# Second down projection of a decoder layer: 16 of 22 k tiles as seven block products

## The reference

```python
def swiglu(x, w_gu, w_down):
    g, u = jnp.split(x @ w_gu, 2, axis=-1)
    return (jax.nn.silu(g) * u) @ w_down

x = x + 0.5 * rms_norm(swiglu(rms_norm(x, pre1), w1_gu, w1_down), post1)
...
x = x + 0.5 * rms_norm(swiglu(rms_norm(x, pre2), w2_gu, w2_down), post2)
```

## Time and profile before

| what | value |
|---|---|
| median of 3 runs | 1167.69 us (1166.46 to 1169.09) |
| the profiled execution | 1168.13 us |
| its span in the trace | 1166.4 us |
| granted TensorE clock, mean | 0.997 of full speed |
| first down stage | about 240 to 360 us |
| second down stage | about 1041 to 1161 us |

### The profile page before, as it was taken

One profiled execution on the slowest core, in us unless ns is written; L12 is line 12 of the kernel. 1 busy time (PEld: TensorE's weight loads), 2 busy tenths in 40 slices (PEclk: granted clock), 3 DMA queues, 4 the chain that ended last, 5 costly groups with the idle time before them and its releaser, 6 DMA issues.

```text
span 1166.4 us, 18885 instructions
## 1 busy us (share of the span) xinstructions
PE 1148.1 (98%) x7220; PEld 1005.9 (86%) x7220; DVE 711.3 (61%) x1153; ACT 519.0 (44%) x972; POOL 94.7 (8%) x198
## 2 busy tenths in 40 slices
PE   8999999999999999999999999999999999999998
PEld 7889999988887888888877888887889999998886
DVE  5888888843316445436886444746598888873233
ACT  6255555632227112247777222335435555552223
POOL 0000000073005100000031100002000000000002
PEclk9999999999999999999999999999999999999999
DMA  7323333347435433471200322232232333342321
GB/s 217 108 66 96 101 101 107 109 164 226 150 108 137 119 97 108 122 240 37 76 3 3 108 72 95 104 108 73 72 108 73 109 108 108 108 147 88 108 72 73
DMA packets 138559, 123.40 MB, mean 106 GB/s; under 512 B 4212, under 2 KB 125212, under 8 KB 138476
## 3 DMA queue, kind: packets, MB, share of 16 engines
q1 hardware_dynamic: 134304, 108.02, 30.7%
q0 software_dynamic: 4080, 14.50, 4.0%
q10 hardware_dynamic: 112, 0.03, 0.0%
HBM read 118.08 MB, written 8.90 MB: 109 GB/s over the span
## 4 chain that ended last, share of the span: by engine, by line
PE 95%; DVE 2%; ACT 1%; issue 1%; DMA 1%; SPq 0%; DVEq 0%; ACTq 0%
PE ps L1793 28%; PE ps L1900 28%; PE ps L1933 21%; PE ps L2038 4%; PE ps L2333 4%; PE ps L2317 2%; PE ps L2169 1%; PE ps L2191 1%; PE ps L2305 1%; PE ps L2100 1%; PE ps L2110 1%; PE ps L2121 1%; ACT p_n L1066 1%; PE ps L2139 1%; PE ps L1817 1%
## 5 line engine op out<-in xcount | busy, mean ns | idle before, releaser
L1190 DVE TENSOR_TENSOR ring_lo<-ring_raw,ring_hi 128x2048 fp32r<-128x2048 f32 (+1 forms) x54 | 121.5, 2252 | 187.4 <-ACT ring_hi L776 187.4
L776 ACT ACTIVATE ring_hi<-ring_raw 128x2048 fp32r<-128x2048 f32 (+1 forms) x54 | 101.5, 1882 | 236.7 <-PE ps L1933 142.0
L1793 PE MATMUL ps<-xn_hi,ring_hi 128*128 128x512 f32 x480 | 189.8, 395 | 2.3 <-DVE xn_lo L1215 2.3
L1793 PE MATMUL ps<-xn_hi,ring_lo 128*128 128x512 f32 x480 | 187.6, 391 | 0.0
L1793 PE MATMUL ps<-xn_lo,ring_hi 128*128 128x512 f32 x480 | 187.5, 391 | 0.0
L1900 PE MATMUL ps<-s_hi,ring_hi 128*128 128x256 f32 x512 | 144.9, 283 | 0.0
L1900 PE MATMUL ps<-s_lo,ring_hi 128*128 128x256 f32 x512 | 144.9, 283 | 0.0
L1900 PE MATMUL ps<-s_hi,ring_lo 128*128 128x256 f32 x512 | 144.9, 283 | 0.0
L1933 PE MATMUL ps<-ring_hi,h_hi 128*128 128x512 f32 x352 | 137.0, 389 | 0.0
L1933 PE MATMUL ps<-ring_hi,hT_lo 128*128 128x512 f32 x352 | 137.0, 389 | 0.0
L1933 PE MATMUL ps<-ring_lo,h_hi 128*128 128x512 f32 x352 | 136.9, 389 | 0.0
(11 more groups left out here) (298 smaller groups left out, 2078.1 us busy)
## 6 DMA issues: line engine op xcount, KB each, us to landing
ring_raw<-in_ffn_w_gu SPq DMA_DIRECT2D x86, 512.0 KB, 4.9
ring_raw<-in_ffn_w_down SPq DMA_DIRECT2D x44, 512.0 KB, 4.2
ring_raw<-in_w_in SPq DMA_DIRECT2D x42, 512.0 KB, 4.7
ring_raw<-in_w_out SPq DMA_DIRECT2D x8, 512.0 KB, 4.1
bias_rows_sparse<-bias_by_distance POOLq DMA_DIRECT2D x1, 2560.0 KB, 15.4
x_tok<-in_x SPq DMA_DIRECT2D x4, 512.0 KB, 6.5
ring_raw<-in_cmp_w_k SPq DMA_DIRECT2D x4, 512.0 KB, 4.5
ring_raw<-in_cmp_w_v SPq DMA_DIRECT2D x4, 512.0 KB, 4.8
```

The source lines that it names most:

```text
L776: e = act.activation(dst, src, ACT.Copy)
L1190: e = dve.tensor_tensor(dst, src, f32(r), ALU.subtract)
L1793: e = pe.matmul(ps[:, 2 * (slot if pair is None else pair) + c, :], part(a, slot, k * 256 + c * P, P), xn[b][:, k, :], start=(k == 0 and i ...
```

## The change

**The second down stage.** The first 16 k tiles are taken as two groups g of 8. In each group h is a 2 x 2 block matrix (256-token row halves x halves of 4 k tiles), and the weights are 2 x 2 blocks of 4 k tiles x 512 columns. Seven products M1 to M7 replace eight. The order is M1, M4, M6, M7, M5, M3, M2, each for g = 0 and 1: 14 ring steps of one weight block (128 x 2048), each with 2 token tiles x 4 k x 3 modes = 24 matmuls of 512 columns. The last 6 k tiles stay classic in three steps (`down_rest`, 48 matmuls each). The second FFN's down stage has 17 ring steps instead of 11.

**h.** DVE forms four sums per group (`sum_h`, 1024 elements per partition) ahead of `lo` in steps 1 to 8. ACT rounds the parts (`hi_part`), DVE takes the differences (`lo_part`).

**PSUM.** Product M1 is copied from banks 0 and 2 to 1 and 3 (ACT, in step 3); M4, M1+M6 and M5 are copied to SBUF (ACT, steps 5, 7, 11); DVE closes the banks with additions (steps 9, 10, 11, 13).

**Weight sums.** Three weight blocks per group are used as they are, four are sums. Pool makes these in the first down stage: it loads the four blocks of a group (1 MB each), makes four sums in place (2048 elements per partition), and stores each to DRAM, first for g = 0, then for g = 1. SP loads them from there as ring steps. Semaphores `vec_stored`, `rows_stored`, `stats_stored` and `c_stored` become one, `scratch_stored`. The first FFN is computed as before.

```diff
-STEPS = FFN2 + UP + DOWN
+STEPS = FFN2 + UP + 17
+M1, M4, M6, M7, M5, M3, M2 = range(7)
+DOWN_STEPS = [(m, g) for m in range(7) for g in range(2)]
+DOWN_BANKS = {M1: (0, 2), M2: (0, 2), M6: (1, 3), M3: (1, 3), M4: (4, 6), M7: (4, 6), M5: (5, 7)}
...
@@ sync
+            def load_down_block(n, w_down, b, g):
+                v = view(n, S)
+                if b in DOWN_SUMS:
+                    sp.wait_ge(sums_stored, 16 * 8)
+                    src = sums_dram[g, DOWN_SUMS.index(b)]
+                else:
+                    k0, c0 = 8 * g + 4 * (BLOCKS[b][1] == "2"), S * (BLOCKS[b][2] == "2")
+                    src = by_k(w_down[k0 * P:(k0 + 4) * P, c0:c0 + S])
+                load(0, n, (v[:, 0:2, :], src[:, 0:2, :]), (v[:, 2:4, :], src[:, 2:4, :]))
...
@@ gpsimd
+            def load_blocks(g):
+                for block_sb, (k_half, c) in zip(blocks_sb, ((0, 0), (0, 1), (1, 1), (1, 0))):
+                    k0 = 8 * g + 4 * k_half
+                    pool.dma_start(block_sb[:, :, :], by_k(w2_down[k0 * P:(k0 + 4) * P, c * S:c * S + S])).then_inc(blocks_loaded, 16)
+
+            def sum_blocks(g):
+                b11, b12, b22, b21 = [b[:, :, :] for b in blocks_sb]
+                t3, t1, t2, t4 = [sums_dram[g, i] for i in range(4)]
+                pool.wait_ge(blocks_loaded, 64 * (g + 1))
+                pool.tensor_tensor(b22, b22, b12, ALU.subtract).then_inc(sum_made, 1)
+                pool.wait_ge(sum_made, 4 * g + 1)
+                pool.dma_start(t3, b22).then_inc(sums_stored, 16)
...
             rows_read(0)
             load_gain(g1_post)
+            load_blocks(0)
...
-            pool.wait_ge(rows_stored, 80)
+            sum_blocks(0)
+            pool.wait_ge(sums_stored, 64)
+            load_blocks(1)
+            pool.wait_ge(scratch_stored, 96)
+            sum_blocks(1)
 
             add_x(0)
+            pool.wait_ge(sums_stored, 128)
...
@@ scalar
+                def hi_part(n):
+                    m, g = DOWN_STEPS[n]
+                    act.wait_ge(*part_event(f, m, g))
+                    act.wait_ge(w_used, base + CLASSIC if n < 2 else first_down + (0 if n < 9 else n - 6 if n < 11 else 2))
+                    act.activation(part_hi[n][:, :, :], part_raw(m, g), ACT.Copy).then_inc(hhi_ready, 1)
...
+                def down_mixed():
+                    hi_part(1)
+                    for n in range(1, 17):
+                        hi(0, first_down + n)
+                        if n == 3:
+                            act.wait_ge(h_ready, UP * (f + 1))
+                            take_product(2, (0, 2), lambda row: ps[:, 1 + 2 * row, :], down_taken)
...
+                        if n < 13:
+                            hi_part(n + 1)
+                        elif n < 16:
+                            hi_rest(n - 13)
...
@@ vector
+                def close_21(row):
+                    bank = ps[:, 4 + 2 * row, :]
+                    dve.wait_ge(w_used, first_down + 8)
+                    dve.wait_ge(down_taken, 4 + row + 1)
+                    dve.tensor_tensor(bank, bank, u2_sb[:, row, :], ALU.add).then_inc(down_closed, 1)
+                    dve.wait_ge(down_closed, 2 * row + 1)
+                    dve.tensor_tensor(u3_sb[:, row, :], bank, m4_sb[:, row, :], ALU.subtract).then_inc(down_closed, 1)
...
+                def down_mixed():
+                    lo_part(1)
+                    first = {1: lambda: sum_h(1, 0), 2: lambda: sum_h(1, 1), 3: lambda: sum_h(2, 0), 4: lambda: sum_h(2, 1),
+                             5: lambda: sum_h(3, 0), 6: lambda: sum_h(3, 1), 7: lambda: sum_h(4, 0), 8: lambda: sum_h(4, 1),
+                             9: lambda: close_21(0), 10: lambda: close_21(1)}
+                    for n in range(1, 17):
+                        if n in first:
+                            first[n]()
+                        lo(0, first_down + n)
+                        if n < 13:
+                            lo_part(n + 1)
+                        elif n < 16:
+                            lo_rest(n - 13)
+                        if n == 11:
+                            for row in range(2):
+                                close_22(row)
+                        if n == 13:
+                            for row in range(2):
+                                close_12(row)
...
@@ tensor
+                def down_product(n):
+                    n0, (m, g) = base + UP + n, DOWN_STEPS[n]
+                    tokens = (part_hi[n][:, :, :], part_low(m, g))
+                    pe.wait_ge(lo_ready, n0 + 1)
+                    pe.wait_ge(hlo_ready, DOWN * f + n + 1)
...
+                    for row, bank in enumerate(DOWN_BANKS[m]):
+                        for k in range(4):
+                            for q, (a, b) in enumerate(MODES):
+                                e = pe.matmul(ps[:, bank, :], tokens[b][:, k, row * P:row * P + P], part(a, ring_slot(n0), k * S, S),
+                                              start=(m in (M1, M4, M5) and g == 0 and k == 0 and q == 0), stop=(g == 1 and k == 3 and q == 2),
+                                              skip_group_check=True)
+                    e.then_inc(w_used, 1)
```

More of the change, by code:

```diff
@@ L105 @@
 X11, S1, S2, X12, S3, X22, S4 = range(7)
+M1, M4, M6, M7, M5, M3, M2 = range(7)
+DOWN_STEPS = [(m, g) for m in range(7) for g in range(2)]
+DOWN_BANKS = {M1: (0, 2), M2: (0, 2), M6: (1, 3), M3: (1, 3), M4: (4, 6), M7: (4, 6), M5: (5, 7)}
+DOWN_SUMS = (T3, T1, T2, T4)
+DOWN_WEIGHTS = {M1: B11, M2: B21, M3: B22, M4: T4, M5: T1, M6: T2, M7: T3}
+H_SUMS = [(which, g) for which in (1, 2, 3, 4) for g in range(2)]
 PAIR_PROJ = CLASSIC
@@ L592, in load_ffn @@
                         load_up(w_gu, base, i, u)
+                if base == FFN2:
+                    for n, (m, g) in enumerate(DOWN_STEPS):
+                        load_down_block(base + UP + n, w_down, DOWN_WEIGHTS[m], g)
+                    for n in range(3):
+                        load_down_rest(base + UP + 14 + n, w_down, 16 + 2 * n)
+                    return
                 load_down(w_down, base + UP, 0, 0)
@@ L1434, in ffn @@
                         mixed(i, u)
-                mixed(MIXED // 2 - 1, 0, ahead=2, extra={"b11": lambda: lo_h(0)})
+                mixed(MIXED // 2 - 1, 0, ahead=2, extra={"b11": lambda: lo_part(0) if f else lo_h(0)})
                 mixed(MIXED // 2 - 1, 1, ahead=1)
[L1437 to L1444, removed]
+                if f:
+                    down_mixed()
+                else:
+                    lo_h(1)
+                    lo(0, first_down + 1)
+                    for n in (2, 3):
+                        lo_h(n)
+                    for n in range(2, DOWN):
+                        lo(0, first_down + n)
+                        if n + 2 < DOWN:
+                            lo_h(n + 2)
                 if p == 0:
@@ new lines, in down_rest @@
+                def down_rest(n):
+                    n0 = base + UP + 14 + n
+                    pe.wait_ge(lo_ready, n0 + 1)
+                    pe.wait_ge(hlo_ready, DOWN * f + 14 + n + 1)
+                    for t in range(NT):
+                        if n == 0:
+                            pe.wait_ge(down_closed, 7 + t if t < 2 else 3 + t)
+                        for c in range(2):
+                            j = 2 * t + c
+                            for kk in range(2):
+                                first = (16 + 2 * n + kk) * S + t * P
+                                tokens = (rest_hi[n][:, kk * S + t * P:kk * S + t * P + P], hT_lo[:, first:first + P])
+                                for q, (a, b) in enumerate(MODES):
+                                    e = pe.matmul(ps[:, j, :], tokens[b], part(a, ring_slot(n0), kk * D + c * S, S),
+                                                  start=False, stop=(n == 2 and kk == 1 and q == 2), skip_group_check=True)
+                            if n == 2 and j < 2 * NT - 1:
+                                e.then_inc(y_done, 1)
+                    e.then_inc(w_used, 1)
@@ L1949, in ffn @@
                     mixed(MIXED // 2 - 1, u, last=u == 1)
-                for n in range(DOWN):
-                    down(n)
+                if f:
+                    for n in range(14):
+                        down_product(n)
+                    for n in range(3):
+                        down_rest(n)
+                else:
+                    for n in range(DOWN):
+                        down(n)
             pe.wait_ge(consts, 5)
```

146 lines of the change are left out of this document (126 added, 20 removed).

## The result

The changed kernel took 1161.21 us (median of 4 runs, 1159.80 to 1163.08), the kernel before 1167.91 (4 runs, 1166.46 to 1169.09): a ratio of 0.9944 [0.9926, 0.9962], so 6.7 us or 0.56% faster. The sum of the prediction was 1161.15, its number 1161.0. The profiled execution took 1163.08 us, the slowest of the four.

What follows compares the result with a forecast made beforehand. TensorE, busy 98% of the span, was taken as the bound. 1168.13 - 10.88 (fewer matmuls) + 0.6 (entry) + 3.3 (handover) = 1161.15 us, 1161.0 as a median; own range 1159 to 1164, low end 1157.0, high end 1168.5.

Steps and rivals of the forecast that it cites:

- 48 matmuls x 226.7 ns: Second down stage: 336 matmuls replace 384 for the sixteen k tiles, saving 10.88 us on TensorE's path.
- The rival of dearer matmuls: Second down stage: 23 ns more on each of 480 matmuls loses the whole gain, 1168 to 1171 us; chance 0.05.
- Entry +0.6: Second down stage's start: `sum_h(1, 0)` ahead of DVE's `lo` makes the second product 0.6 us late, between 0 and 1.4.
- No wait in products 2 to 13: Second down stage: no gap after the one before the second product; TensorE waiting there would prove the prediction wrong.
- the rival of the ring: Second down stage: loads landing in 7.2 us pace the products, costing 5 us and giving 1166; chance 0.08.
- The sum of 2048 elements: Pool in the first down stage: one weight sum estimated at 4.6 us, upper end 5.2.
- The handover: First down stage's end to the projections: Pool's fourth sum holds DVE's PROJ halves, idling TensorE for 3.3 us.
- The start of batch 1: First down stage: Pool's second group of four sums starts at 331.5; outside 326 to 337 the prediction is wrong.
- Pool is ready in time: First down stage: rival with faster 4 MB transfers or 4.2 us sums, so no handover loss; 1157.9 us, chance 0.25.
- The hold in the first down stage: Pool's sums holding DVE's `lo` within the stage: taken as 0, with 2 us as the end.
- The clock: Loss of clock after a TensorE gap: named only for the far-too-late case, with no row to price it.
- the very long gap: Handover: rival with Pool far too late, `add_x` starting 15.3 us past the 354.7 that cost nothing; 1173 us, chance 0.08.

Runs made afterwards that it cites:

- the reordered kernel: Changed kernel with the four sums of group 0 and the loads of group 1 moved ahead of the five bias row copies; 1156.48 us, ratio 0.9903.
- the repeat: The changed kernel run once more as it is, on the chip of the next runs; 1161.53 us, ratio 0.9950.
- the kernel without the last sum: Changed kernel with only the last of Pool's eight additions left out, its block stored unsummed; 1157.92 us, ratio 0.9916.
- half sums: Changed kernel with each Pool sum made as two instructions of half the width; one execution, 1162.47 us.
- Pool's work alone: Kernel before plus Pool's loads, sums and stores, which nothing reads, with the second down stage as before; 1170.34 us, ratio 1.0018.
- both reordered ones: The reordered kernel (1156.48 us), and the same with DVE's `lo` ahead of the sum of h in steps 1 and 2 (1156.17 us).

## Why the prediction was right, step by step

- **48 matmuls x 226.7 ns: held.** 480 remain in the second down stage, at their old duration; the stage is 10.05 us shorter (119.72 and 109.67), and 10.9 once the entry (0.95 us between two starts, then 0.33, where 0.23 is the plain distance: 0.8 in all) is taken off. The rival of dearer matmuls falls.
- **Entry +0.6: held, a little small.** The list of waits gives 0.6, before the second product alone, and the stage is 0.8 longer for it. The cause is the one named: changing the order of `lo` and the sum took 0.5 of it away.
- **No wait in products 2 to 13: held.** TensorE has none there, and DVE's sum of h takes 1.22 us for 1.23. DVE was idle 0.9 to 1.1 us in each of steps 3 to 8, where the text had 0.7, and about 0.6 in steps 9 and 10, where it had 0.5. The ring's loads from the sums landed in 4.0 us in the median against the 4.2 taken: the rival of the ring falls.
- **The sum of 2048 elements: held.** 4.62 us for the estimate of 4.6.
- **The handover: held nearly to the tenth.** In the prediction's order: third sum ended 348.5 (348.48), fourth 353.9 (353.98), last issue 354.7 (354.8), halves 356.2 (356.2), Pool's adds 357.8 to 362.9 (357.73 to 362.73), first PROJ matmul 367 (367.50). Counted from the first down stage's start, the handover cost about 3.05 for the 3.3 of the sum. Leaving out the fourth sum shows the cause. The rule on the shared port pair (the Trainium skill, page "SBUF — State Buffer", section "SBUF: two separate sides") is that the one of the two that starts first has the pair for its whole instruction. That the other stands for the whole instruction is borne out in both directions: 6.14 us for a Pool sum behind a DVE subtraction, 6.68 for a DVE subtraction behind a Pool sum; and with no additions on Pool nothing was held. That the first to start gets it is not borne out by the recorded starts (last section).
- **The start of batch 1: 330.2 for 331.5, but by terms that cancel.** The issues of the first loads did not delay the row copies by 3.2 us: the 107 copies that follow took 21.0 us instead of 24.1, the last row copy was issued at 274.57 (before 275.02). Batch 0 then took its 23.5 us (23.7 in the text) and ended at 299.1, not 303. The stores were done 11.1 us later, at 310.2, not 13.2 later at 316. Then the loads took 20.1 us from their first issue where 15 were allowed. One term out by five, made good by 3.7 and 2.1 the other way; with loads of 15 batch 1 would have begun at 325, and the case "Pool is ready in time" (from before 328) would have come true. The Trainium skill's rule for one transfer on this path (page "DMA: Bandwidth & Descriptors", section "Anatomy of one DMA — SWDGE (gpsimd) path") is about 2.0 us plus the bytes over 436 GB/s; taken over all 4 MB it gives an estimate of 11.6 us. The trace does not agree: 20.1 here, 16.8 in the reordered kernel (296.20 to 312.96), with the ring's loads beside them.
- **The hold in the first down stage: missed, +0.8.** It stood at 0 with an end of 2, on the argument that `lo` waits for one sum in a step with 6.4 us of air. The argument left out that `hT_lo`, also a difference of two SBUF tiles, is on the same queue. DVE lost four times in a row: `lo` 7.97, `hT_lo` 5.65, `lo` 6.68, and `hT_lo` again 5.65 us. Two steps' air went in 20 us, and TensorE waited 0.5 by its list (0.8 in the repeat), which made the stage 0.8 longer. In the reordered kernel DVE lost three times in a row, twice (6.39, 5.64, 6.68 and 6.93, 5.65, 6.68 us), and TensorE did not wait.
- **The clock: not priced, 1.6 us in the profiled execution.** The text named a loss of clock only for the very long gap. It came with a gap of ordinary length too (the kernel without the last sum).

- **Small slips of the text.** Its own two figures put ACT 0.13 us behind the last matmul of step 0, not 0.3; and it takes 0.15 off its sum to get 1161.0 as a median, where its first paragraph names 0.4. Neither changes the forecast.

The terms that were missed come to 2.4 us (the hold 0.8, the clock 1.6), the entry was 0.2 dearer, the handover 0.25 cheaper, and the first down stage began 0.44 earlier; so the profiled execution (1163.08) is above the sum by 1.9. The median of four is 1161.21 nonetheless, 1.9 below the profiled run, whereas before the profiled run stood 0.2 above its median (1167.91). So the agreement to 0.2 us is luck, of which executions were profiled and of two missed terms that the median hides. What is sound is the mechanism: the products, the entry and the handover each came within 0.3 us of their price in the traces, the handover with inner terms that cancel.

The cases where Pool is in time were worked out at 1157.9, 1157.5 as a median. Four kernels of that kind came out at 1156.1 to 1156.6, about 1 us less. Their profiles show the second handover (from 810 us) at full clock, where the kernel before and the changed one lose 1.5 us (10.04 and 10.06 us from the first PROJ matmul to the 54 that follow, 8.50 in the reordered kernel); whether that belongs to them or to the executions profiled, the runs don't settle.

## What to carry to other kernels

An idle engine is free only if it shares nothing: in this kernel additions of two SBUF tiles on Pool hold DVE's differences of two SBUF tiles for their whole length (6.68 us for one of 2.29), so count every such instruction on DVE's queue, and put Pool's ahead of a stretch with air, never where DVE's results open the next stage. Where a chain of load, sum and store shares a queue with bulk copies that are wanted later, issue the chain first: that move was worth 4.7 us here (1161.21 to 1156.48), beside 6.7 for the whole change. And when a step gets half as long, look again at the order within each engine's step: 0.5 of the 0.8 us of the entry was one pair of DVE instructions in the wrong order.

## What the runs showed of the hardware that was not expected

**DVE is held although it began first.** In the kernel after, DVE's `lo` began at 274.42 and the Pool sum at 275.14 in the records, yet DVE stood until the sum ended (7.97 us; 280.23 + 2.16 = 282.39), and the sum took 5.09 instead of 4.62. In the reordered kernel 318.30 and 318.45 gave 6.93. At 329.60 and 330.22 it was the other way round: Pool stood, 6.14 us. So the recorded starts alone don't say who waits. It is not Pool's issuing of DMAs, under which DVE kept its 2.29 us; the cause was not tried further and stays open.

**They take turns, mostly.** Through batch 0 each DVE instruction lets one sum pass and each sum one DVE instruction (5.09, 5.77, 4.66, 5.76 us on Pool). With half sums this does not always hold: some DVE instructions stood for one half (4.49 us), others through both (8.00, 7.38, and 5.13 for the PROJ half). Why was not tried.

**The clock behind a handover does not follow from the work there.** Behind the first: low in the changed kernel, its repeat, Pool's work alone, and the kernel without the last sum, which has no longer gap than the kernel before; with half sums it was 0.50 from 362 on. Full in the kernel before, without Pool's work, without additions, and in both reordered ones. Behind the second, where the code of all is the same, two windows of the kernel before are at

```profile
810.00:812.00 2.00, 1.76 (x5) 1.47 (x6) 2.00 (x4) 2.00 (x3) 0.00 (x0) 0.65 0.00 0
812.00:814.00 2.00, 2.00 (x7) 1.50 (x7) 1.19 (x2) 1.54 (x2) 0.00 (x0) 0.50 0.00 0
```

and the changed kernel, its repeat and Pool's work alone are low there too (their first six matmuls in 2.44 to 2.59 us), while the kernels without Pool's work, without additions, without the last sum, with half sums, and the reordered ones run them in 1.62 to 1.63. Where the clock fell behind a handover, it cost 1.5 to 1.6 us up to the 54 matmuls that follow (1.8 with half sums). Whether it fell can't be told from how long TensorE had stood: the kernel before and the kernel without the last sum stood alike at the first handover, at full clock in one and not in the other. One profile doesn't settle it.
